# Products of the identity with itself behind the last output product and behind the second transposes of each block end

## What is computed

```python
def reference(x, ...):
    x = first_block(x, ...)
    return second_block(x, mem_2, ...)

def second_block(x, mem, ...):
    for i in range(DEPTH_2):
        x = layer_norm(ALPHA * x + 0.5 * swiglu(x, ffn1_w_gate[i], ffn1_w_up[i], ffn1_w_down[i]),
                       ln_g[i, 0], ln_b[i, 0])
        ...
        x = layer_norm(ALPHA * x + heads @ w_out[i], ln_g[i, 1], ln_b[i, 1])
        x = layer_norm(ALPHA * x + 0.5 * swiglu(x, ffn2_w_gate[i], ffn2_w_up[i], ffn2_w_down[i]),
                       ln_g[i, 2], ln_b[i, 2])
    return x
```

## Time and profile before

| | us |
|---|---|
| median of three runs | 1634.25 |
| lowest, highest | 1630.90, 1635.93 |
| profiled execution | 1636.34 |
| its span, first to last instruction | 1634.60 |

### The profile page before, as it was taken

The page is one execution under the profiler, slowest core; times in us unless marked ns, Lnnn a source line. Parts: engine busy times, 40 slices in busy tenths (PEclk is TensorE's granted clock), DMA queues, the critical chain, the costliest instruction groups (busy, mean ns, idle before and its releaser), DMA issues. The chain is left out here.

```text
span 1634.6 us, 30766 instructions
## 1 busy us (share of the span) xinstructions
PE 1460.2 (89%) x12484; PEld 1328.6 (81%) x12484; DVE 958.9 (59%) x1213; ACT 675.2 (41%) x848; POOL 231.0 (14%) x208
## 2 busy tenths in 40 slices
PE   5999799997999978939867999979999895799997
PEld 4777699996999968828856999969999794589997
DVE  2665576666555565674538555585555547475556
ACT  4445455444333345542324333343334445343332
POOL 1440132220000024002303000030000302030000
PEclk8999999998999989969978999989999897789999
DMA  9954466663666644300024666656665440366662
GB/s 362 345 178 186 129 204 190 190 181 106 192 192 180 181 137 143 114 1 4 4 77 130 193 185 187 180 149 185 182 191 168 155 155 1 103 202 180 182 188 95
DMA packets 297827, 257.71 MB, mean 158 GB/s; under 512 B 6928, under 2 KB 274192, under 8 KB 294672
## 3 DMA queue, kind: packets, MB, share of 16 engines
q1 hardware_dynamic: 297744, 256.49, 50.7%
HBM read 255.42 MB, written 1.05 MB: 157 GB/s over the span
## 5 line engine op out<-in xcount | busy, mean ns | idle before, releaser
L137 PE MATMUL ps<-actT,a_parts 128*128 128x256 f32 x2176 | 626.3, 288 | 22.0 <-DVE actT L399 10.4
L138 PE MATMUL ps<-actT,a_parts 128*128 128x256 f32 x2176 | 622.5, 286 | 0.0
L139 PE MATMUL ps<-actT,a_parts 128*128 128x256 f32 x2176 | 622.2, 286 | 0.0
L137 PEld LDWEIGHTS ps<-actT,a_parts 128*128 128x128 f32 x2176 | 424.4, 195 | 33.4 <-issue 18.4
L138 PEld LDWEIGHTS ps<-actT,a_parts 128*128 128x128 f32 x2176 | 424.6, 195 | 3.6
L139 PEld LDWEIGHTS ps<-actT,a_parts 128*128 128x128 f32 x2176 | 424.4, 195 | 0.0
L1111 DVE TENSOR_TENSOR a_parts<-a_raw,a_parts 128x2048 fp32r<-128x2048 f32 x100 | 239.7, 2397 | 72.9 <-ACT a_parts L1108 72.7
L1108 ACT ACTIVATE a_parts<-a_raw 128x2048 fp32r<-128x2048 f32 x100 | 190.0, 1900 | 0.0
L1125 DVE TENSOR_TENSOR b_parts<-b_raw,b_parts 128x1024 fp32r<-128x1024 f32 x72 | 88.3, 1226 | 154.3 <-ACT b_parts L1122 154.3
L1122 ACT ACTIVATE b_parts<-b_raw 128x1024 fp32r<-128x1024 f32 x90 | 95.1, 1057 | 175.8 <-PE ps L139 175.8
L137 PE MATMUL ps<-b_parts,hid 128*128 128x512 f32 x400 | 157.8, 394 | 6.3 <-DVE hid L1192 6.3
(11 more groups left out here) (343 smaller groups left out, 1801.0 us busy)
## 6 DMA issues: line engine op xcount, KB each, us to landing
a_raw<-in_ffn_w_gate SPq DMA_DIRECT2D x88, 512.0 KB, 3.9
a_raw<-in_ffn_w_up SPq DMA_DIRECT2D x88, 512.0 KB, 5.1
b_raw<-in_ffn_w_down SPq DMA_DIRECT2D x88, 512.0 KB, 3.2
arena<-in_mod_w SPq DMA_DIRECT2D x24, 1024.0 KB, 8.9
a_raw<-in_f_up_w SPq DMA_DIRECT2D x44, 512.0 KB, 4.9
b_raw<-in_f_down_w SPq DMA_DIRECT2D x22, 512.0 KB, 3.2
a_raw<-in_rwkv_w_in SPq DMA_DIRECT2D x10, 1024.0 KB, 5.2
a_raw<-in_sb_w_in SPq DMA_DIRECT2D x10, 1024.0 KB, 5.4
```

Of the source, the lines that this page charges most:

```text
L137: pe.matmul(out, lhs[0], rhs[0], start=start, stop=False)
L138: pe.matmul(out, lhs[0], rhs[1], start=False, stop=False)
L139: return pe.matmul(out, lhs[1], rhs[0], start=False, stop=stop)
```

## The change

A helper `keep_busy(pe, n)` issues n products of the 128 x 128 float32 identity with itself into the first 128 columns of PSUM bank 1. They wait for nothing and signal nothing, and nobody reads what they write. Fourteen stand at the end of TensorE's list in the blocks `ffn`, `ffn1` and `ffn2` of layer 0, `ffn1` of layer 1 and the two output stages, behind the last output product; seven stand behind the eight transposes with which TensorE starts the block that follows each of these. That makes six places with 14 and 7 products. The last feed-forward ends without them.

```diff
@@ -358,6 +358,11 @@
             if i and t == 0 and k >= 6:
                 return ps[:, 0, (k - 6) * P:(k - 5) * P]
             return turned_tok[:, t, k]
+
+        def keep_busy(pe, n):
+
+            for _ in range(n):
+                pe.matmul(ps[:, 1, 0:P], ident[:], ident[:], start=True, stop=True)
 
         def turn_tokens(pe, i, t):
 
@@ -1229,6 +1234,7 @@
                 def _(pe):
                     if take is not None:
                         turn_tokens(pe, got, 1)
+                        keep_busy(pe, 7)
                     up_pe(pe, 0, 0)
                     up_pe(pe, 1, 0)
                     down_pe(pe, 0, 0, True, False)
@@ -1258,6 +1264,8 @@
                             ins.then_inc(ring_b.used, 1)
                         elif tile == tiles[-1]:
                             ins.then_inc(acc_done, 1)
+                    if not last:
+                        keep_busy(pe, 14)
 
                 @block.scalar
                 def _(act):
```

## The result

The changed kernel takes 1638.61 us (median of 20 executions, 1633.65 to 1642.45); the kernel before, on the same chips, 1634.55 us (20 executions, 1630.62 to 1637.73). The ratio is 1.0022, 95% interval 1.0012 to 1.0032: **slower, by about 3.6 us of 1634**, where -0.3 us was forecast. The time lies 0.1 us above the top of my range. The profiled execution took 1639.47 us (span 1637.5).

A forecast was written before the change was run, and what follows sets the result against it. TensorE was taken as the bound, busy 89% of the span, at half clock around six block ends. Terms -1.8 + 0 - 2.3 + 1.8 + 0.2 + 1.8 = -0.3 us against 1634.25 gave 1634.0 us, range 1628 to 1638.5.

The forecast's parts named there:

- Length of the fillings: At the block ends: 14 products, 28 records at 0.109 us, take 3.05 us of 3.56 free; 7 take 1.5 us.
- B: Block end at 595 us, to the RWKV projection: 0, bounds 0 to -2.5 us; third chunk waits for its load.
- F: Block end at 1430 us, output stage to the last ffn2: the same as C, +1.8 us.
- R2: Rival, 7%: records cost 0.19 us, 14 products take 5.3 us and delay the block's end at six places: 1644.5 us.
- They hold the clock: TensorE's longest idle time at the block ends shrinks from 3.8 to about 0.9 us, so full clock through them.
- R3: Rival, 7%: identity products don't hold the clock and the half-clock stretches stay: 1636.5 us.
- A: Block end at 390 us, first feed-forward to ffn1 of layer 0: full clock in the 96 products, -1.8 us.
- E: Block end at 1279 us, to the stick projection: clock -2.6, start -0.36, second token pair +0.7, together -2.3 us.
- C: Block end at 877 us, output stage to ffn2: start -0.36, down products at half clock +2.15, together +1.8 us.
- D: Block end at 1077 us, to ffn1 of layer 1: -0.36 + 2.15 - 1.6 (already paid before), +0.2 us.
- R1: Rival, 18%: the clock survives 3.5 us idle ahead of the down products, the gain stays: 1628.3 us.
- The price: Down products at C, D, F: 0.465 us lost per us at half clock, 2.15 us at the mean 4.6 us.

The follow-up runs named there:

- E alone: Identity products at block end E only (14 and 7), against the kernel before the change: 1633.07 us, ratio 0.9989.
- The parts timed apart: Three kernels with identity products at A and E only, at C, D and F only, and at B only, against the kernel before: -4.0, +4.8 and -0.2 us.
- A and E alone: Identity products at block ends A and E only (14 and 7 at each), against the kernel before the change: 1631.28 us, ratio 0.9979.

## Why the prediction was right or wrong, step by step

- **Length of the fillings: right.** 28 records recorded as 3.29 us, the last of them 0.28 long, have 3.01 us from the first start to the last, 27 steps of 0.112 us, and 14 have 1.45. So 28 take 3.12 and 14 take 1.56, against 3.05 and 1.5. (They write a quarter of the bank, 128 of its 512 columns, and not the half that I wrote.) Every block ends as early as before; at B to F the restart comes 6.12 to 6.21 us behind the first transposes in all kernels. R2 is out.
- **They hold the clock: right.** It is 1.00 from the filling to the first products at all six places. R3 is out. The page "TensorE: Matmul & The Clock Gate" of the Trainium skill, section "Part 4: PE-mode transpose", says that a transpose doesn't count as busy for the clock in the way a product does. Eight of them between two fillings, 1.06 us, did no harm here, which is too short a stretch to decide on it.
- **A, -1.8: right,** -1.78 in every profile with its fillings, and the fillings that began at half clock cost at most 0.1 us between the last product and the transposes (4.44 to 4.51 us, 4.44 before). The fall behind the first transposes, which I had left as it was, was missing in both profiles of the changed kernel, and the block end at A took 6.5 us instead of 7.6. It was missing in the kernel with E alone too, which has no filling at A, and there in six other kernels that have one; I take it for chance.
- **Start at C, D, F, -0.36: right** (-0.33: 3.64 to 3.31).
- **The longer idle time and the fall at C, D and F: right.** Idle 3.48 us where 3.5 was forecast, half clock behind it at all three, in every profile without the 14 products. R1 is out. The price is right in sum and unevenly spread: against the kernels without a fall a fall cost 1.6 us at C (195.29 less 193.72) and D, with 3.4 us at half clock, and 2.8 at F with 6.8. That is 0.46 and 0.41 per us, beside my 0.465. So C came out at +1.2, not +1.8, D at -0.4, not +0.2, and F at +2.5, not +1.8. Together +3.3 by the profile against +3.8, and +4.8 ± 0.8 timed. I had said C and F would each be slower by about 2; with eight, seven and twelve slow products of twelve, "ten or more" held only at F.
- **E, -2.3: wrong, and this is the step that failed.** It got -0.2, in two profiles of the changed kernel (-0.3 at the last of the 96 products). Two terms of it were at fault. The start: I carried C's 0.36 us over to E, but GpSimd's list goes on differently there. Behind the split stand five short instructions that at C don't exist, and they took the time back: the first product comes 3.87 us behind the transposes, 0.19 later than before instead of 0.36 earlier. And the wait: I had counted the second token pair as +0.7 us of time, not as idle time for the clock. With 1.25 us ahead of the first product and 0.39 six products later the clock fell again, in the stretch for which I had booked the gain, 1.5 us. I knew both rows; I did not ask of each new wait, as I did at C, what it does to the clock. With the five instructions out of the way the gain at the last of the 96 is 2.4 us: the size was right for the start that I had assumed.
- **B, 0 with a gain of up to 2.5 as the other end: sign of the bound wrong.** The executions say 0 to +2, the profiles near +2. I had bounded it by the clock, and the risk was VectorE's split against GpSimd's residual.
- **The sum.** With E at -0.2 instead of -2.3 and F, C and D as measured, my sum is -1.8 + 0 - 0.2 + 1.2 - 0.4 + 2.5 = +1.3, and with B's +0.9 the +2.2 of the profiles. Of the 2.5 us that this lies above my -0.3, E is 2.1, B 0.9 and F 0.7, with C and D 0.6 each the other way. The change was timed at +3.6 ± 0.7 in the first series and +2.1 ± 1.0 in the second; up to 1.4 us of it I can't place. The parts timed apart give -4.0 + 4.8 - 0.2 = +0.6 ± 1.9, 2.4 to 3 us less than the whole; E kept its clock in the profile of A and E alone and lost it in those of the whole, which is 1.7 us of that at the last of its 96 products (15.80 against 17.49). What then is left is within the errors.

## What to carry to other kernels

Work that keeps the clock up pays only if what runs right behind it is waited for. A stage that ends in a wait for another engine turns a faster clock into a longer wait, and the longer wait can cost the clock where it counts; so fill the wait directly ahead of the paid work first (here 21 products for -2.4 ± 0.8 us), and the others after it. Look at more than one profile of each kernel before you explain a us or two: here the clock fell or held at D and at E in kernels that were the same there. When tokens are to be ready earlier, read the other engines' lists for what now falls beside the instruction that makes them.

## What the runs showed of the hardware

- A product of two float32 128 x 128 operands, recorded twice, takes 2 x 0.112 us from start to start at full clock (28 records in the changed kernel), and such products hold the clock although nothing is done with their result.
- The clock's fall is not decided by the length of the wait alone. It held through 1.75 us at C before and through 1.24 + 0.39 us in the kernel with E alone, and fell after 1.25 + 0.39 us in two profiles of the changed kernel. After 3.48 us it fell at fifteen places of fifteen, in the five profiles with fillings at C, D and F and none ahead of the down products; with 14 products in that wait it held at twelve of twelve, in four profiles.
- A float32 cast of 128 x 256 on VectorE took 0.29 us by itself and 0.61 to 1.14 us while GpSimd split tokens and wrote memsets. The Trainium skill, page "Advanced Engine Details and Errata", section "VectorE Performance Modes", states that VectorE's second SBUF port is shared with GpSimd, and that GpSimd's instructions and those of VectorE that use both ports block each other. No run shows which ports this cast uses; the rows fit such blocking, and show that either engine may be the one that is held up (a memset took 0.46 us instead of 0.31, a residual instruction 4.4 instead of 2.3).
